# First products of a decoder step in another order, with their loads issued by two engines, and another order of the first head pair's units

## The chip, the cores and the metric

One core of one Trainium2 chip runs the whole program. The time is device microseconds of that core for one execution; less is better. The median of three runs of the kernel before is 1621.52 us.

## What is computed

One layer of a decoder step: 1,024 prompt tokens and 32 sample tokens (8 sequences of 4), model width 1,024. The reference, cut to what this case touches:

```python
d = x @ w_a_down                       # 1024 -> 384 (query) + 256 (latent) + 32 (rotary key)
c_q, c_kv, k_r = rms_norm(d[:384]), rms_norm(d[384:640]), rope(d[640:])
q = (c_q @ w_a_uq)                     # 16 heads of 64 + 32
k_nope = einsum('bsc,chd->bshd', c_kv, w_a_uk)
v      = einsum('bsc,chd->bshd', c_kv, w_a_uv)
p = softmax(mask((q_nope @ k_nope + q_rope @ k_r) * scale))
o = p @ v
```

The sample tokens attend to a paged cache in the latent space instead; then follow the output product, a layer norm, a gated ConvFFN and a second norm. Only the first 120 us of the program are touched here.

## The kernel before, in words

Products of prompt tokens are made of three matmuls each: both factors are split into a high part in a narrower format and the rest as a low part, and high x high, high x low and low x high are added in PSUM. ScalarE makes a high part (a copy) and VectorE the low part (a subtraction) out of it, so each operand goes through ScalarE, then VectorE. Weights, activations and intermediate results are all treated so. The eight PSUM banks are handed out by hand, and counters (semaphores) order the engines; each engine has its own list of instructions, in an order written out by hand, so a wait holds back all that stands behind it on that engine.

**project** (from L128). The 1,056 tokens are nine tiles (TILES): first the sample tile of 32 tokens, then eight of 128. For a tile, transpose_x turns x (eight transposes), ScalarE and VectorE split it, and `products` multiplies it with the down weight of 8 chunks k by 672 columns in two halves: six matmuls for a k. The sample tile is multiplied unsplit in down_samples: for each of the eight k, four matmuls side by side, each on a 32-column strip of the array, into bank 2. The first prompt tile (down_first) is multiplied while the weight's halves are made: its step k waits for chunk k to be split by ScalarE (L425) and VectorE (L513), and the next tile's transposes stand before step 6. SyncE issues the loads: the sample tile (128 KB), weight chunk 0 (336 KB), the first prompt tile (512 KB), chunks 1 to 7, and the next two x tiles. TensorE's list is: transposes of tiles 0 and 1, down_samples, down_first, transposes of tile 3, the next tile's products. At the end of the stage TensorE computes six units of the first head pair ahead ("early": v0, k0, q00, q10, q01, q11), each into its own bank.

**attend** (from L643). Eight head pairs, each with 16 score units; the projections of a pair are units too: v0, v1 (values transposed, 512 tokens each), k0, k1 (keys), q and two digits (head 0 or 1, third of the tokens 0, 1 or 2; one third is 352 columns, and third 2 has the sample tokens), wt (a transposed key weight), t0, t1 (values turned back), ql. A k unit is taken by ScalarE (k_hi, two copies) and VectorE (k_low, two subtractions); a q unit by VectorE (q_scale, out of the bank), ScalarE (q_high) and VectorE (q_low). q_high of third 2 has three small copies for the sample tokens before its own. The q units pass through two buffers, qf, in turn. For the first pair, FIRST is the order on TensorE, FIRST_TAKEN the order in which they are counted when taken, FIRST_BANK the bank and FIRST_AFTER the unit whose taking frees it. On entry TensorE computes wt, v1, k1, q02, q12, then scores(0, 0), which needs q02 split. The score unit n uses banks 0 and 1 for even n, 2 and 3 for odd n; scores of n = 2 need exp of n = 0. VectorE takes the row maximum, ScalarE the exponential.

```python
FIRST_BANK = {"v0": 0, "k0": 1, "q00": 4, "q10": 5, "q01": 2, "q11": 3, "wt": 6, "v1": 7, "k1": 1, "q02": 6, "q12": 0}
FIRST_AFTER = {"k1": "k0", "q02": "wt", "q12": "v0"}
```

## Time and profile before

| | |
|---|---|
| median of 3 runs | 1621.52 us (1621.4 to 1621.68) |
| profiled execution, its own time | 1620.46 us |
| its span in the trace | 1618.8 us |
| granted TensorE clock, mean | 0.998 |
| TensorE busy | 98% |
| VectorE, ScalarE, GpSimd busy | 58%, 36%, 12% |
| DMA, mean | 67 GB/s |

The span goes from the first to the last instruction. A busy share is an average; what a stretch is worth is read from the timeline of that stretch. In a timeline, "[1.62 <-DVE k_lo L1005]" behind an instruction says how long its engine was idle before it and which instruction's end released it. PE is TensorE's matmuls, PEld its weight loads, which overlap them; DVE is VectorE, ACT ScalarE, POOL GpSimd, SPq SyncE's queue.

### The profile page before, as it was taken

The numbers are of one execution on the slowest core, as the hardware profiler recorded it, in microseconds if no ns is written. First come the engines' busy times: TensorE is split into PE (matmuls) and PEld (weight loads), VectorE is DVE, ScalarE is ACT, GpSimd is POOL, SyncE is SP. The second block draws the span as 40 slices with busy tenths as digits, with TensorE's granted clock in tenths as the row PEclk, the third lists the DMA queues.
The fourth block names the chain that finished last, engine by engine and source line by source line (L and its number), as shares of the span: only waits on it lengthen the run. The fifth ranks groups of instructions, "written<-read, shape, count | busy, mean of one in ns | idle before, by whom it ended". The sixth has DMA issues, their size and how long they took to land. (4 is left out here: it accounts for less than half of the span.)

```text
span 1618.8 us, 29618 instructions
## 1 busy us (share of the span) xinstructions
PE 1584.5 (98%) x10341; PEld 1404.1 (87%) x10341; DVE 938.0 (58%) x1818; ACT 586.1 (36%) x1281; POOL 192.3 (12%) x297
## 2 busy tenths in 40 slices
PE   8989999999999999999999999999999999999998
PEld 7978888888886566657889999999999999999996
DVE  5665666656665655555766465545555554465547
ACT  5455655556554333332233131121302213131136
POOL 2000000000000430000003021120211202121000
PEclk9999999999999999999999999999999999999999
DMA  6111111011113765533113020220202112020103
GB/s 225 42 31 31 29 23 25 12 28 26 29 46 115 237 207 170 171 114 95 39 59 111 27 65 13 65 65 26 63 15 65 47 31 65 26 65 13 40 27 118
DMA packets 150583, 109.18 MB, mean 67 GB/s; under 512 B 54623, under 2 KB 139293, under 8 KB 150352
## 3 DMA queue, kind: packets, MB, share of 16 engines
q1 hardware_dynamic: 148704, 102.17, 21.4%
q0 software_dynamic: 1776, 5.71, 1.1%
q8 instruction: 56, 0.92, 0.2%
q14 instruction: 47, 0.39, 0.1%
HBM read 101.88 MB, written 10.14 MB: 69 GB/s over the span
## 5 line engine op out<-in xcount | busy, mean ns | idle before, releaser
L1950 PE MATMUL banks<-act_hi,up_hi 128*128 128x352 f32 (+2 forms) x1040 | 335.5, 323 | 0.7 <-PEq L1522 0.7
L1951 PE MATMUL banks<-act_lo,up_hi 128*128 128x352 f32 (+2 forms) x1040 | 335.1, 322 | 0.0
L1952 PE MATMUL banks<-act_hi,up_lo 128*128 128x352 f32 (+2 forms) x1040 | 334.9, 322 | 0.0
L1950 PEld LDWEIGHTS banks<-act_hi,up_hi 128*128 128x128 f32 x1040 | 195.5, 188 | 1.0 <-issue 0.9
L1951 PEld LDWEIGHTS banks<-act_lo,up_hi 128*128 128x128 f32 x1040 | 195.4, 188 | 0.0
L1952 PEld LDWEIGHTS banks<-act_hi,up_lo 128*128 128x128 f32 x1040 | 195.2, 188 | 0.0
L2253 DVE TENSOR_TENSOR o_t<-o_t,banks 128x352 f32<-128x352 f32 x240 | 121.0, 520 | 94.5 <-PE banks L1952 94.2
L2232 DVE SCALAR_TENSOR_TENSOR conv_out<-conv_in,conv_now,conv_out 128x1072 f32<-128x1072 f32 x42 | 63.7, 1517 | 185.7 <-ACT conv_out L2106 185.7
L1027 DVE TENSOR_REDUCE neg_max<-banks 128x1 f32<-128x896 f32 (+7 forms) x128 | 96.7, 756 | 115.6 <-PE banks L810 115.0
L2097 ACT ACTIVATE conv_in<-banks 128x352 f32<-128x352 f32 x84 | 36.2, 457 | 336.0 <-PE banks L1952 336.0
L1950 PE MATMUL banks<-gated_hi,down_hi 128*128 128x352 f32 x480 | 155.8, 325 | 0.0
L1951 PE MATMUL banks<-gated_lo,down_hi 128*128 128x352 f32 x480 | 154.3, 321 | 0.0
L1952 PE MATMUL banks<-gated_hi,down_lo 128*128 128x352 f32 x480 | 154.2, 321 | 0.0
L903 ACT ACTIVATE probs<-banks,neg_max 128x896 f32<-128x896 f32 (+7 forms) x128 | 94.5, 738 | 42.9 <-DVE inv_rows L1037 24.6
L1950 PEld LDWEIGHTS banks<-gated_hi,down_hi 128*128 128x128 f32 x480 | 90.1, 188 | 1.3
L1951 PEld LDWEIGHTS banks<-gated_lo,down_hi 128*128 128x128 f32 x480 | 90.2, 188 | 0.0
L1952 PEld LDWEIGHTS banks<-gated_hi,down_lo 128*128 128x128 f32 x480 | 90.1, 188 | 0.0
L821 PE MATMUL banks<-ident,probs 128*128 128x128 f32 x576 | 87.0, 276 | 2.6 <-DVE probs_t L1048 2.4
L732 PE MATMUL banks<-k_hi,q_hi 128*128 128x512 f32 (+2 forms) x192 | 71.9, 375 | 10.6 <-DVE q_scaled L1012 6.2
L839 PE MATMUL banks<-probs_t,v_rows 128*64 128x256 f32 (+1 forms) x640 | 72.8, 365 | 0.8 <-DVE probs_t L1048 0.8
L2235 DVE SCALAR_TENSOR_TENSOR conv_out<-conv_in,conv_now,conv_out 128x1072 f32<-128x1072 f32 x42 | 69.3, 1651 | 1.5
L821 PEld LDWEIGHTS banks<-ident,probs 128*128 128x128 f32 x576 | 62.0, 141 | 6.5 <-DVE probs_t L1048 4.4
(339 smaller groups left out, 3084.1 us busy)
## 6 DMA issues: line engine op xcount, KB each, us to landing
weight_stage<-in_w_f_up SPq DMA_DIRECT2D x44, 512.0 KB, 4.7
c_stage<-in_cache_kv_latent SPq DMA_DIRECT2D x140, 128.0 KB, 2.2
down_stage<-in_w_f_down SPq DMA_DIRECT2D x22, 512.0 KB, 4.3
head_weights_stage<-in_cache_kv_latent SPq DMA_DIRECT2D x56, 128.0 KB, 2.1
rope_query_tab<-in_cache_kv_latent SPq DMA_DIRECT2D x56, 128.0 KB, 2.2
o_t<-in_x_prompt SPq DMA_DIRECT2D x8, 512.0 KB, 4.2
rope_rows<-in_cache_k_rope SPq DMA_DIRECT2D x256, 16.0 KB, 1.9
wo_stage<-in_w_a_out POOLq DMA_DIRECT2D x8, 512.0 KB, 4.5
```

Source lines behind the costliest of these rows:

```text
L732: nc.tensor.matmul(o, ws[0], xs[0], start=first, stop=False)
L821: last = nc.tensor.transpose(ps[:, 4 + t % 2, k * P:(k + 1) * P], prob[:, n % 2, c + k * P:c + (k + 1) * P], m.ident[:, :])
L839: last = nc.tensor.matmul(ps[d, 6, q], v[:, j, d], pt[:, g % 2, hh, j, q], start=j == 0, stop=j == 2 * g + 1)
L903: nc.scalar.activation(prob[:, n % 2, 0:wd], src, ACT.Exp, bias=nmax[:, n % 2:n % 2 + 1], accum_out=sums[:, n % 2:n % 2 + 1]).then_inc(pr, 1)
L1027: nc.vector.tensor_reduce(nmax[:, n % 2:n % 2 + 1], src, axis=AXX, op=ALU.max, negate=True).then_inc(nm_ok, 1)
L1950: nc.tensor.matmul(o, ws[0], xs[0], start=first, stop=False)
L1951: nc.tensor.matmul(o, ws[0], xs[1], start=False, stop=False)
L1952: return nc.tensor.matmul(o, ws[1], xs[0], start=False, stop=last)
L2097: nc.scalar.activation(u[i][:, 2 + CH * c:2 + CH * c + CH], src, ACT.Copy).then_inc(ev, 1)
L2232: nc.vector.scalar_tensor_tensor(out=v[i][:, 0:CW], in0=u[i][:, 1:UW - 1], scalar=cwi[:, 1, i, j:j + 1], in1=v[i][:, 0:CW], op0=ALU.mult, ...
L2235: nc.vector.scalar_tensor_tensor(out=v[i][:, 0:CW], in0=u[i][:, 0:UW - 2], scalar=cwi[:, 0, i, j:j + 1], in1=v[i][:, 0:CW], op0=ALU.mult, ...
L2253: nc.vector.tensor_tensor(y, y, ps[:, 4 + unit % 4, 0:CH], ALU.add).then_inc(add, 1)
```

## The change

At the start, SyncE keeps the loads of the sample tile, of weight chunk 0 and of chunks 3 to 7; ScalarE issues those of the first prompt tile and of chunks 1 and 2, ahead of its first copy. On TensorE down_samples and down_first become steps of one k: after sample steps 0 to 4 prompt step 0 follows, then sample step 5, prompt step 1, and so on; prompt steps 4 to 7 come last.

At the entry of attention TensorE's order becomes wt, k1, q02, q12, v1, t0, scores(0, 0). k1 goes to v0's bank, q02 to bank 7, q12 to k0's bank, v1 to wt's bank. VectorE scales q01 and q11 first, before k0; it scales all q units before the first row maximum. ScalarE makes the high parts of q01 and q11 ahead of k1; the small copies for the samples move behind both high parts of third 2, and v1 is taken last. k_low's first half starts when the first half of k_hi is done. The scores wait for q02 alone (n = 0) and for q12 (n = 2).

```diff
--- before.py
+++ after.py
@@ -176,24 +176,25 @@
...
+        def load_x(eng, i):
+            t = TILES[i]
+            src = io["x_prompt"][0, t * P:(t + 1) * P, :] if t < TT - 1 else io["x_sample"].rearrange("b t d -> (b t) d")
+            eng.dma_start(x[0:rows(t), i % 2, :], src).then_inc(x_in[i % 2], 16)
+        def load_w(eng, k):
+            eng.dma_start(wst[k], io["w_a_down"][k * P:(k + 1) * P, :]).then_inc(w_in[k], 16)
...
-            def load_x(i):
-                t = TILES[i]
-                src = io["x_prompt"][0, t * P:(t + 1) * P, :] if t < TT - 1 else io["x_sample"].rearrange("b t d -> (b t) d")
-                sp.dma_start(x[0:rows(t), i % 2, :], src).then_inc(x_in[i % 2], 16)
-            def load_w(k):
-                sp.dma_start(wst[k], io["w_a_down"][k * P:(k + 1) * P, :]).then_inc(w_in[k], 16)
-            load_x(0)
-            load_w(0)
-            load_x(1)
-            for k in range(1, KD):
-                load_w(k)
+            load_x(sp, 0)
+            load_w(sp, 0)
+            for k in range(3, KD):
+                load_w(sp, k)
...
-                load_x(i)
+                load_x(sp, i)
...
@@ -206,7 +207,7 @@
...
-                    load_x(i + 3)
+                    load_x(sp, i + 3)
...
@@ -268,29 +269,29 @@
...
-            def down_samples():
-                pe.wait_ge(xt_hi, 2)
+            def down_samples(k):
+                pe.wait_ge(w_in[k], 16)
...
-                for k in range(KD):
-                    pe.wait_ge(w_in[k], 16)
-                    for g in range(4):
-                        last = nc.tensor.matmul(ps[32 * g:32 * g + 32, 2, 0:n], xs[:, k, :], wst[k][:, g * n:(g + 1) * n],
-                                                start=k == 0, stop=k == KD - 1)
-                last.then_inc(d_ps, 1)
-            def down_first():
-                pe.wait_ge(xt_hi, 4)
-                pe.wait_ge(xt_lo, 2)
-                for k in range(KD):
-                    if k == KD - 2:
-                        transpose_x(2)
-                    pe.wait_ge(w_hi, k + 1)
-                    pe.wait_ge(w_lo, k + 1)
-                    products(1, 0, k)
-                    last = products(1, 1, k)
-                last.then_inc(d_ps, 1)
+                for g in range(4):
+                    last = nc.tensor.matmul(ps[32 * g:32 * g + 32, 2, 0:n], xs[:, k, :], wst[k][:, g * n:(g + 1) * n],
+                                            start=k == 0, stop=k == KD - 1)
+                if k == KD - 1:
+                    last.then_inc(d_ps, 1)
+            def down_first(k):
+                if k == 0:
+                    pe.wait_ge(xt_hi, 4)
+                    pe.wait_ge(xt_lo, 2)
+                if k == KD - 2:
+                    transpose_x(2)
+                pe.wait_ge(w_hi, k + 1)
+                pe.wait_ge(w_lo, k + 1)
+                products(1, 0, k)
+                last = products(1, 1, k)
+                if k == KD - 1:
+                    last.then_inc(d_ps, 1)
...
@@ -341,8 +342,12 @@
...
-            down_samples()
-            down_first()
+            pe.wait_ge(xt_hi, 2)
+            for k in range(KD + 4):
+                if k < KD:
+                    down_samples(k)
+                if k >= 4:
+                    down_first(k - 4)
...
@@ -415,6 +420,9 @@
...
+            load_x(act, 1)
+            for k in (1, 2):
+                load_w(act, k)
...
@@ -538,8 +546,8 @@
...
-FIRST_BANK = {"v0": 0, "k0": 1, "q00": 4, "q10": 5, "q01": 2, "q11": 3, "wt": 6, "v1": 7, "k1": 1, "q02": 6, "q12": 0}
-FIRST_AFTER = {"k1": "k0", "q02": "wt", "q12": "v0"}
+FIRST_BANK = {"v0": 0, "k0": 1, "q00": 4, "q10": 5, "q01": 2, "q11": 3, "wt": 6, "v1": 6, "k1": 0, "q02": 7, "q12": 1}
+FIRST_AFTER = {"k1": "v0", "v1": "wt", "q12": "k0"}
...
@@ -590,8 +598,8 @@
...
-FIRST = ["v0", "k0", "q00", "q10", "q01", "q11", "wt", "v1", "k1", "q02", "q12", "t0", "t1", "ql"]
-FIRST_TAKEN = ["v0", "k0", "wt", "v1", "k1", "q02", "q12", "q01", "q11", "q00", "q10", "t0", "t1", "ql"]
+FIRST = ["v0", "k0", "q00", "q10", "q01", "q11", "wt", "k1", "q02", "q12", "v1", "t0", "t1", "ql"]
+FIRST_TAKEN = ["v0", "q01", "q11", "k0", "k1", "wt", "q02", "q12", "v1", "q00", "q10", "t0", "t1", "ql"]
...
@@ -658,6 +666,7 @@
...
+        qs_ok = s("q_samples_ok")
...
@@ -747,7 +756,7 @@
...
-                    bank_free(p, "q10" if p else "v1")
+                    bank_free(p, "q10" if p else "q02")
...
@@ -778,7 +787,7 @@
...
-                    pe.wait_ge(qn_ok, p + 1)
+                    pe.wait_ge(qn_ok, 2 * p + 2)
...
@@ -796,9 +805,9 @@
...
-                if n == 1 and p == 0:
-                    pe.wait_ge(pj_dve, dve_count(0, "q11"))
-                if n % 4 == 0 and g >= 1:
+                if n in (0, 2) and p == 0:
+                    pe.wait_ge(ql_ok, 3 + n // 2)
+                elif n % 4 == 0 and g >= 1:
...
@@ -858,6 +867,7 @@
...
+            project_unit(0, OWN_AT[0])
...
@@ -874,7 +884,7 @@
...
-                    if n in OWN_AT:
+                    if n in OWN_AT and p + n:
...
@@ -935,22 +945,24 @@
...
-                copy(m.khi[0:NOPE, 0, c], src[0:NOPE, :])
+                copy(m.khi[0:NOPE, 0, c], src[0:NOPE, :]).then_inc(kh_ok, 1)
...
+            def q_samples(p, name):
+                hh, i, at = int(name[1]), place_in(p, name, Q_UNITS) % 2, SEQ - 2 * CH
+                for part in range(2):
+                    r0 = (NOPE, 0)[hh] + part * ROPE
+                    copy(m.qr[0:ROPE, part, :, (2 * p + hh) * DEC_SEQ:(2 * p + hh + 1) * DEC_SEQ],
+                         qf[r0:r0 + ROPE, i, at:CH].rearrange("p (b t) -> p b t", t=DEC_SEQ)).then_inc(qs_ok, 1)
+                rows_ = slice(hh * NOPE, (hh + 1) * NOPE)
+                copy(qn[rows_, hh * N_SAMPLE:(hh + 1) * N_SAMPLE], qf[rows_, i, at:CH]).then_inc(qn_ok, 1)
...
-                if name[2] == "2":
-                    at = SEQ - 2 * CH
-                    for part in range(2):
-                        r0 = (NOPE, 0)[hh] + part * ROPE
-                        copy(m.qr[0:ROPE, part, :, (2 * p + hh) * DEC_SEQ:(2 * p + hh + 1) * DEC_SEQ],
-                             qf[r0:r0 + ROPE, i, at:CH].rearrange("p (b t) -> p b t", t=DEC_SEQ))
-                    rows_ = slice(hh * NOPE, (hh + 1) * NOPE)
-                    last = copy(qn[rows_, hh * N_SAMPLE:(hh + 1) * N_SAMPLE], qf[rows_, i, at:CH])
-                    if hh:
-                        last.then_inc(qn_ok, 1)
+                if name[2] == "2" and p:
+                    q_samples(p, name)
...
@@ -960,13 +972,17 @@
...
-            for name in FIRST_TAKEN[:len(EARLY) - 2]:
-                if name in BY_ACT:
-                    take(0, name)
-                elif name[0] == "k":
-                    k_hi(0, name)
-                else:
-                    q_high(0, name)
+            take(0, "v0")
+            k_hi(0, "k0")
+            q_high(0, "q01")
+            q_high(0, "q11")
+            k_hi(0, "k1")
+            take(0, "wt")
+            q_high(0, "q02")
+            q_high(0, "q12")
+            q_samples(0, "q02")
+            q_samples(0, "q12")
+            take(0, "v1")
...
@@ -998,10 +1014,12 @@
...
-                dve.wait_ge(kh_ok, 2 * p + place_in(p, name, ("k0", "k1")) + 1)
+                halves = 4 * p + 2 * place_in(p, name, ("k0", "k1"))
+                dve.wait_ge(kh_ok, halves + 1)
...
+                dve.wait_ge(kh_ok, halves + 2)
...
@@ -1009,6 +1027,9 @@
...
+                if p == 0 and name in ("q00", "q10"):
+                    dve.wait_ge(qn_ok, int(name[1]) + 1)
+                    dve.wait_ge(qs_ok, 2 * int(name[1]) + 2)
...
@@ -1059,19 +1080,19 @@
...
+            q_scale(0, "q01")
+            q_scale(0, "q11")
...
+            q_low(0, "q01")
+            q_low(0, "q11")
...
-            q_scale(0, "q01")
-            q_scale(0, "q11")
-            row_max(0, 0)
-            q_low(0, "q01")
-            q_low(0, "q11")
...
+            row_max(0, 0)
...

```

## Rows read from the trace of the kernel before

**Rows 1.** The page's busy part: share of the span that TensorE is busy.
```profile
PE 1584.5 (98%) x10341; PEld 1404.1 (87%) x10341; DVE 938.0 (58%) x1818; ACT 586.1 (36%) x1281; POOL 192.3 (12%) x297
```

**Rows 2.** TensorE's waits, whole span: us in total, times, longest us.
```profile
...
PE banks L732 <- DVE q_scaled L1012: 6.2, 7, 0.9
...
PE banks L732 <- DVE q_lo L1018: 3.3, 1, 3.3
...
PE banks L732 <- DVE k_lo L1005: 1.6, 1, 1.6
```

**Rows 3.** Busy time of PE, PEld, DVE, ACT, POOL; PEclk, DMA share, GB/s.
```profile
...
40.00:60.00 20.00, 20.00 (x145) 19.97 (x143) 12.81 (x57) 9.83 (x30) 0.00 (x0) 1.00 0.22 68
```

**Rows 4.** Timeline of the start, TensorE: start us, us, what, xcount.
```profile
6.37 1.97 PE L256 MATMUL banks<-ident,o_t 128*128 128x128 f32 x8 [1.72 <-DMA o_t<-in_x_prompt]
...
8.27 1.48 PEld L278 LDWEIGHTS banks<-o_t,x_samples_t 128*32 128x32 f32 x32 [0.33 <-ACT xt_hi_tile L380]
...
10.09 0.16 PEld L278 LDWEIGHTS banks<-o_t,x_samples_t 128*32 128x32 f32 x8 [0.34 <-DMA o_t<-in_w_a_down]
...
12.67 0.16 PEld L278 LDWEIGHTS banks<-rope_query_tab,x_samples_t 128*32 128x32 f32 x8 [0.68 <-DMA rope_query_tab<-in_w_a_down]
...
13.10 0.42 PE L267 MATMUL banks<-wdown_hi,xt_hi_tile 128*128 128x336 f32 x1
...
22.29 0.40 PE L267 MATMUL banks<-wdown_hi,xt_hi_tile 128*128 128x336 f32 x1
```

**Rows 5.** The same timeline, ScalarE and VectorE: the weight's halves.
```profile
8.87 3.37 ACT L425 ACTIVATE wdown_hi<-o_t 128x672 fp32r<-128x672 f32 x5
...
9.66 3.93 DVE L513 TENSOR_TENSOR wdown_lo<-o_t,wdown_hi 128x672 fp32r<-128x672 f32 x5
```

**Rows 6.** GB/s moved in 40 slices of 0.35 us, 0 to 14 us.
```profile
GB/s 0 0 0 0 0 187 125 232 123 300 320 388 327 363 413 386 346 307 269 307 399 376 407 384 346 384 438 384 415 438 384 430 412 422 394 433 410 421 421 375
```

**Rows 7.** The same timeline, SyncE's issue of the first prompt tile.
```profile
1.80 0.43 SPq L184 DMA_DIRECT2D o_t<-in_x_prompt  x1
```

**Rows 8.** Timeline of attention's entry, TensorE.
```profile
95.27 0.42 PE L767 MATMUL banks<-ident,head_weights_stage 128*128 128x128 f32 x2 [0.33 <-PEq L126]
...
98.71 0.50 PE L732 MATMUL banks<-ck_hi,wk_hi 128*128 128x512 f32 x1 [1.62 <-DVE k_lo L1005]
...
100.19 0.32 PE L732 MATMUL banks<-cq_hi,wq_hi 128*128 128x352 f32 x1
...
106.52 0.47 PE L732 MATMUL banks<-k_hi,q_hi 128*128 128x512 f32 x1 [3.26 <-DVE q_lo L1018]
...
107.88 0.45 PE L732 MATMUL banks<-k_hi,q_hi 128*128 128x512 f32 x1
...
109.38 0.61 PE L779 MATMUL banks<-ident,v_t 128*128 128x128 f32 x4
110.36 0.50 PE L732 MATMUL banks<-k_hi,q_hi 128*128 128x512 f32 x1 [0.37 <-ACT probs L903]
...
113.33 0.50 PE L732 MATMUL banks<-k_hi,q_hi 128*128 128x512 f32 x1 [0.65 <-ACT probs L903]
```

**Rows 9.** The same stretch, ScalarE.
```profile
95.95 1.18 ACT L893 ACTIVATE k_hi<-banks 64x512 fp32r<-64x512 f32 x2
...
103.60 0.47 ACT L893 ACTIVATE q_rope<-q_scaled 32x32 f32<-32x32 f32 x2 [2.01 <-DVE q_scaled L1012]
...
104.22 0.48 ACT L893 ACTIVATE q_hi<-q_scaled 128x352 fp32r<-128x352 f32 x1
...
109.21 1.01 ACT L903 ACTIVATE probs<-banks,neg_max 128x896 f32<-128x896 f32 x1
```

**Rows 10.** The same stretch, VectorE.
```profile
97.96 0.69 DVE L1005 TENSOR_TENSOR k_lo<-banks,k_hi 64x512 fp32r<-64x512 f32 x1
...
103.05 0.96 DVE L1012 TENSOR_TENSOR q_scaled<-banks,rope_query_tab 128x352 f32<-128x352 f32 x2
...
108.08 1.09 DVE L1027 TENSOR_REDUCE neg_max<-banks 128x1 f32<-128x896 f32 x1 [0.84 <-PE banks L810]
```

## Prediction

> **What bounds the kernel now.** I read the page first: TensorE is busy 98% of the span [rows 1], so time can only be won where it stands still. Its waits say where [rows 2]: 3.3 and 1.6 us once each, at one place, and 6.2 us in seven waits that come back in each later head pair, which the change leaves alone. The windows by stage show TensorE full from 40 to 60 us, 20.00 of 20.00 [rows 3]; the projection after the first prompt tile is TensorE's own work, so what is won ahead of it arrives at attention, and what is won at attention's entry arrives at the end, provided no other engine becomes late.
>
> The timeline of the start [rows 4] shows the first stretch. The prompt tile's transposes begin at 6.37, released by its load. The weight loads of the sample products begin at 8.27, and those of chunks 0 to 3 (32 loads) are through in 1.48 us; chunk 4's wait until 10.09 for its load, the last chunk's until 12.67, so the sample products follow the DMA. Only at 13.10 do the prompt tile's products begin. Yet their operands are there earlier [rows 5]: ScalarE splits chunk 0 from 8.87, VectorE from 9.66, five low halves in 3.93, so 0.79 each, and the first is ready at about 10.5.
>
> The second stretch is attention's entry [rows 8]: k1 waits 1.62 us for its bank, which VectorE frees by taking k0 until about 98.65 [rows 10]; the first scores wait 3.26 us for q02's low half; then 0.37 and 0.65 us for the first two exponentials. From 113.33 TensorE goes on with no wait of that size.
>
> **The start, step by step.** The number of instructions on TensorE stays. What changes is which of them fill the wait: prompt step 0 begins at a time F in place of 13.10. From 13.10 the eight prompt steps and two groups of transposes last until 22.29, 9.19 us [rows 4]. After the change three sample steps (5, 6, 7) lie in between. What one costs there is not in the trace; the bounds are 0.37 (1.48 / 4, steps back to back) and 0.85 (0.43, the isolated last step from 12.67 to 13.10, plus 0.42, one product that nothing overlaps, for emptying the array both ways). I take 0.53: the isolated step, plus the 0.10 by which the first product after it (0.42) is longer than a similar one in a stream (0.32, [rows 8]). That row is nearest, because it is the same change of shape. Sum: start gain = 13.10 - F - 3 x 0.53 = 11.5 - F.
>
> F is the later of two: the low half of chunk 0, and the end of sample step 4. Today they would be 10.5 and 10.09 + 0.43 = 10.5. Now the loads. ScalarE has nothing to do at the start and issues the prompt tile beside SyncE's first load, which is two issues (0.43 each, with a little between) ahead of 1.80 [rows 7]: 0.9 earlier. If transfer followed issue, everything behind it would be 0.9 earlier: F = 9.6. The DMA row speaks against it [rows 6]: from the slice at 3.15 us on it moves 300 to 430 GB/s without a hole, so the loads are limited by bytes there, not by issue. Up to 3.15 us it moved 0.35 x (187 + 125 + 232 + 123) = 233 KB, where the later rate would give about twice that; a second queue can fill half of that hole, about 0.4 us. So I put the prompt tile at 0.4 us earlier, and the halves of chunk 0 at 10.1.
>
> Chunks 1 and 2 stand behind the prompt tile on ScalarE's queue, while SyncE's goes on with 3, 4 and so on. With chunks 0 to 4, the sample tile and the prompt tile 2.3 MB are to be moved either way; chunk 2 was ready after 1.65 MB (128 + 512 + 3 x 336 KB), and if the two queues share evenly it is ready only after about 2.3 MB. At 400 GB/s that is 1.6 us later, less the 0.4. As chunk 4 (the 2.3 MB today) came at 10.09, chunk 2 comes at about 9.6, and sample steps 2, 3 and 4 follow it in 3 x 0.37: F = 10.6. ScalarE reaches chunk 2 at 8.87 - 0.4 + 2 x 0.67 = 9.8 and is not held back, nor is VectorE, whose low halves (0.79 each) run ahead of TensorE's prompt steps. **Start gain 0.9 us**; bounds 13.10 - 9.6 - 3 x 0.37 = 2.4 and, with chunk 2 at 10.1 and steps of 0.85, 13.10 - 11.2 - 2.55 = -0.7.
>
> By the Trainium skill (DMA: Bandwidth & Descriptors, "Queues, rings and completion order" and "Issuing engines are not separate DMA queues") SP's and ACT's loads share the same 16 engines, which take turns between the queues packet by packet, so a second issuer saves issue time only. By it chunk 2 comes late as above and the start gives about 0.9 us; by issue times alone it would give 13.10 - 9.6 - 1.6 = 1.9 us. Rows 6 side with the rule on the bytes; no row shows two such queues at once.
>
> The three DMA issues cost ScalarE 3 x 0.43 = 1.3 us in a stretch in which it waits for the first transposes anyway; only if its table load no longer fitted there would that cost something. SyncE is free earlier and issues the tile after next earlier; its bytes stand behind chunk 7 and are wanted only near 17 us. Edits at no cost: the second semaphore on k_hi, separate counts for the sample copies and the load helpers add no instruction that works, and in later pairs the order is the old one.
>
> **The entry of attention.** Times here are on the old scale. TensorE: wt at 95.27; k1 needs v0's bank, which ScalarE leaves when it turns to k0 at 95.95 [rows 9], so k1 at about 96.05 and 1.48 long [rows 8]; q02 and q12 1.46 each (100.19 to the end of both at about 103.1), v1 1.48 like k1, t0 0.5: scores(0, 0) can begin at 96.05 + 1.48 + 2.92 + 1.48 + 0.5 = 102.45. Nobody holds that up by more: VectorE scales q01 and q11 until 96.5 (0.96 a pair, [rows 10]), takes k0 behind ScalarE's halves (0.59 each) until 98.0, so q12's bank is free 1 us before TensorE wants it at 99.0; low halves of q01 and q11 until 98.95, k1 until 100.35 (1.39 for both halves), scales q02 and q12 until 101.3. ScalarE makes k1's high halves until 99.3 and takes wt at 99.65, so v1's bank is free 0.8 us early; then q02 high until 101.4 (0.48, without the 0.62 of sample copies that stood ahead of it, [rows 9]), and VectorE's q02 low half is done at about 102.0, 0.45 us ahead of TensorE. So v1 and t0, 1.98 us of work that was elsewhere, now cover this wait. Scores begin at 102.45 in place of 106.52: 4.07 us earlier.
>
> Then the maximum (108.08 today, 1.56 after the scores' start) at 104.0; VectorE's scales of q00 and q10 wait for the sample copies (two times 0.62 from 101.9) and end at 103.7, in time. The exponential (109.21) starts at 105.2, the third scores (110.36) at 106.3, and the fourth (113.33) at about 108.95, because the second maximum no longer stands behind two scale steps: **entry gain 4.2 us**, 4.07 to 4.4. As a check, the removed waits add to 1.62 + 3.26 + 0.37 + 0.65 = 5.9, and new ones of 0.5 (v0's bank), 0.9 and 0.4 (the exponentials) remain: 4.1. What is late next is the exponential, whose table load and row maximum end together. Bounds: 4.9 if one of the new waits goes too, 3.0 if TensorE stands 1.2 us at q02's low half, twice the handoff margin that I find.
>
> **Sum.** 0.9 + 4.2 = 5.1 us. The profiled execution took 1620.46, span 1618.8; it becomes 1615.4. The median of the runs stands 1.1 above it, 1621.52, so I say 1616.4. About 0.2%, 3.2 us, is what a measurement of this kernel can tell from no change.
>
> **Rivals.** (a) The start gives nothing, the entry all: chunk 2 late by the full 1.6 us and sample steps at 0.8; start between -0.7 and 0.4. For it: no row shows a mixed order of steps. Against it: prompt step 0 starts at least 1.9 us earlier in every bound. Time 1621.5 - 4.2 + 0.2 = 1617.5; 20%. The Trainium skill (TensorEngine Tiling (Array Packing), "Key Properties") says that a change of tiling mode drains TensorE, which is this rival's mechanism. (b) A handoff between ScalarE and VectorE stays at the entry, since seven follow one another there with margins under 1 us: entry 2.3, start 0.9, 1618.3; 11%. (c) Loads follow issue, and the sample steps are cheap: start 2, entry 4.3, 1615.2; 10%. (d) Slower than before: the DMA engines serve ScalarE's queue last. The prompt tile then lands behind 2.8 MB of SyncE's loads, at about 14 us instead of 6.37; prompt step 0 follows 4.1 us later at 18, with all chunks there: start 11.5 - 18 = -6.5, entry 4.2, time 1623.8. It decides against the change once the tile lands after 11.6 us. Against it: nothing in the rows, only that both queues are filled by the same kind of issue; 3%. (e) The gain doesn't reach the end, because a later stage hangs on loads or on GpSimd that start at fixed times: 1621; 3%. Against it, all loads there wait for TensorE's or VectorE's counts. The forecast itself has 53%.
>
> **How the numbers follow.** Cases (c), forecast, (a) and (b) span 1615.2 to 1618.3; with the bounds of the forecast (start 0.3 to 1.7, entry 3.7 to 4.6) 1615.2 to 1617.5. I give 1614.7 to 1618.6, leaving out (d), (e) and the tails of (a) and (b). Faster by over 0.2% means under 1618.3: the forecast, (c), most of (a) and about half of (b), 0.85; same 0.12; slower 0.03, half of (d) and what I don't see.
>
> **What would show it.** At the start: the prompt tile's transposes near 6.0; prompt step 0 between 10 and 11; three sample steps between prompt steps, 0.5 each; tile 2's products 0.9 earlier than 22.29. At the entry, against its own first instruction: k1 after 0.8 us, no idle time until the first scores 7.2 us after it, k1's bank wait and q02's low half gone from the list of waits, two exponentials still in it. If the first scores wait for q_lo, (b) holds; if prompt step 0 starts before 10, loads follow issue; if the transposes begin after 12, (d). I am wrong in the main if the entry gives under 3 us, or if the gain seen at 115 us is not there at the end.

## The result: 8.6 us less, where 5.1 were forecast

| | before | after |
|---|---|---|
| median of 4 runs each, one chip | 1621.58 us | 1612.98 us (1610.44 to 1613.67) |
| profiled execution, its span | 1620.46, 1618.8 us | 1613.67, 1612.0 us |
| granted TensorE clock, mean | 0.998 | 0.997 |

The ratio is 0.9947 (0.9934 to 0.9959). The change is faster, as forecast, but by more than the range of 1614.7 to 1618.6 us held.

The page's busy part of the kernel after has the instruction counts of [rows 1], nothing added or taken away, and TensorE at 98% as before:

```profile
PE 1586.9 (98%) x10341; PEld 1406.4 (87%) x10341; DVE 939.3 (58%) x1818; ACT 585.6 (36%) x1281; POOL 191.0 (12%) x297
```

TensorE's waits over the whole span of the kernel after (what was waited for: us in total, times, longest us):

```profile
PE banks L257 <- DMA o_t<-in_x_sample: 4.5, 1, 4.5
PE banks L830 <- DVE probs_t L1069: 2.3, 6, 0.4
PE banks L741 <- DVE q_scaled L1033: 1.9, 7, 0.3
...
PE banks L741 <- ACT probs L913: 1.3, 2, 1.1
PE banks L848 <- DVE probs_t L1069: 1.2, 1, 1.2
...
PE banks L741 <- ACT v_t L903: 0.4, 1, 0.4
PE banks L277 <- DMA o_t<-in_w_a_down: 0.4, 1, 0.4
```

Beside [rows 2]: the waits of 3.3 and 1.6 us are gone, as they should be. But the seven waits for q_scaled went from 6.2 to 1.9 us, and the forecast had them untouched.

**Where the time went.** I take four marks in the two traces and subtract. TensorE's first product of the third tile, 22.29 before and 21.65 after: 0.65 us won at the start. Attention from its first instruction on TensorE to decoding's first product (500.12 before, 491.99 after): 404.85 and 397.37, so 7.48 us won. From there to the first product of the next stage (742.48 and 735.66): 242.36 and 243.67, 1.31 lost. The rest is the same within 0.1 us, and TensorE is full from 40 to 60 us as in [rows 3]. 0.65 + 7.48 - 1.31 = 6.8, the difference of the spans. The medians differ by 8.6; a stretch at half clock that the profiled execution of the kernel before happens to lack may account for about one of the 1.8 us between them (part 2 of the experiments).

**The start**, TensorE's timeline of the kernel after (start us, us, what, xcount, idle time before and what released it):

```profile
9.17 1.49 PE L277 MATMUL banks<-o_t,x_samples_t 128*32 128x168 f32 x24 [0.37 <-DMA o_t<-in_w_a_down]
10.59 0.42 PE L268 MATMUL banks<-wdown_hi,xt_hi_tile 128*128 128x336 f32 x1
...
11.71 0.49 PE L277 MATMUL banks<-rope_query_tab,x_samples_t 128*32 128x168 f32 x8
12.13 0.42 PE L268 MATMUL banks<-wdown_hi,xt_hi_tile 128*128 128x336 f32 x1
...
21.65 0.40 PE L268 MATMUL banks<-wdown_hi,xt_hi_tile 128*128 128x336 f32 x1
```

Against [rows 4]: chunk 2 is late, its sample step waits until 9.17, and prompt step 0 begins at 10.59 instead of 13.10 (10.6 was forecast). Then each pair of a sample step and a prompt step takes 12.13 - 10.59 = 1.54 us, of which six products are 0.93 in a stream (11.16 - 10.85 is 0.31 for two of them), so a sample step in between costs 0.61 and not the 0.53 that I took. That prompt step 0 begins on time is in part luck: chunk 2 came 0.4 earlier than forecast, and the three sample steps behind it took 1.42 for 1.1. The queue of ScalarE issues the prompt tile at 0.87, for 1.80 in [rows 7]:

```profile
0.87 0.42 ACTq L183 DMA_DIRECT2D o_t<-in_x_prompt  x1
```

**Attention's entry**, the same view:

```profile
94.62 0.41 PE L776 MATMUL banks<-ident,head_weights_stage 128*128 128x128 f32 x2 [0.33 <-PEq L126]
95.45 0.50 PE L741 MATMUL banks<-ck_hi,wk_hi 128*128 128x512 f32 x1 [0.42 <-ACT v_t L903]
...
101.60 0.47 PE L741 MATMUL banks<-k_hi,q_hi 128*128 128x512 f32 x1
...
105.72 0.50 PE L741 MATMUL banks<-k_hi,q_hi 128*128 128x512 f32 x1 [1.09 <-ACT probs L913]
...
108.07 0.50 PE L741 MATMUL banks<-k_hi,q_hi 128*128 128x512 f32 x1
```

From its first instruction, k1 comes after 0.83 us, the first scores after 6.98 without a wait (11.25 before, [rows 8]), the fourth after 13.45 (18.06 before). ScalarE and VectorE show what is late next:

```profile
103.27 1.28 ACT L913 ACT_TABLE_LOAD   x1
104.56 1.01 ACT L913 ACTIVATE probs<-banks,neg_max 128x896 f32<-128x896 f32 x1
```
```profile
103.27 1.08 DVE L1048 TENSOR_REDUCE neg_max<-banks 128x1 f32<-128x896 f32 x1
```

The exponential starts when its table is loaded, 0.21 us after the row maximum is done; v1 was taken just ahead of the load. This is the 1.09 us of TensorE's wait.

**The boundary between two pairs**, which recurs seven times. VectorE and TensorE before:

```profile
154.28 0.68 DVE L1004 TENSOR_TENSOR k_lo<-banks,k_hi 64x512 fp32r<-64x512 f32 x1 [2.54 <-ACT k_hi L893]
154.97 0.69 DVE L1005 TENSOR_TENSOR k_lo<-banks,k_hi 64x512 fp32r<-64x512 f32 x1
...
156.47 0.95 DVE L1012 TENSOR_TENSOR q_scaled<-banks,rope_query_tab 128x352 f32<-128x352 f32 x2
```
```profile
157.03 0.50 PE L732 MATMUL banks<-k_hi,q_hi 128*128 128x512 f32 x1 [0.88 <-DVE q_scaled L1012]
```

ScalarE's two copies to k_hi there run from 153.05 for 1.20 us, and VectorE idles 2.54 us until both are done, although its first subtraction needs the first alone. Behind them stand an inverse, its copy and a step of o_t, and only then the scaling of q00, for which TensorE's next scores wait. After the change (the next boundary, VectorE, GpSimd and TensorE):

```profile
198.54 0.68 DVE L1021 TENSOR_TENSOR k_lo<-banks,k_hi 64x512 fp32r<-64x512 f32 x1 [1.94 <-ACT k_hi L903]
199.24 0.69 DVE L1023 TENSOR_TENSOR k_lo<-banks,k_hi 64x512 fp32r<-64x512 f32 x1
...
200.16 0.19 DVE L1058 COPY inv_rows<-inv_sums 128x64 f32<-128x64 f32 x1
...
200.72 0.94 DVE L1033 TENSOR_TENSOR q_scaled<-banks,rope_query_tab 128x352 f32<-128x352 f32 x2
...
201.77 0.75 DVE L1058 COPY inv_rows<-inv_sums 128x64 f32<-128x64 f32 x1
```
```profile
201.65 0.83 POOL L587 CAST wq_hi<-head_weights_stage 128x768 fp32r<-128x768 f32 x1
```
```profile
201.29 0.50 PE L741 MATMUL banks<-k_hi,q_hi 128*128 128x512 f32 x1 [0.27 <-DVE q_scaled L1033]
```

VectorE starts one copy, 0.60 us, earlier, and TensorE's wait falls from 0.88 to 0.27. The pair period (the distance from one pair's transposes of the key weight to the next pair's) is 50.59 before and 50.15 after.

**Behind attention** the windows (us; busy time of PE, PEld, DVE, ACT, POOL with counts; granted clock, DMA share, GB/s) show the loss, before and after:

```profile
500.00:501.00 1.00, 0.88 (x6) 0.87 (x6) 0.00 (x0) 0.00 (x0) 0.00 (x0) 0.90 0.00 0
501.00:504.00 3.00, 3.00 (x15) 2.94 (x16) 1.22 (x4) 1.04 (x4) 1.68 (x4) 0.50 0.78 243
504.00:505.00 1.00, 1.00 (x10) 1.00 (x9) 0.39 (x1) 0.57 (x1) 0.53 (x1) 0.89 0.91 293
```
```profile
491.00:492.00 1.00, 0.01 (x1) 0.04 (x1) 0.42 (x1) 0.14 (x1) 0.00 (x0) 0.69 0.00 0
492.00:498.00 6.00, 6.00 (x27) 5.87 (x28) 1.91 (x5) 1.61 (x4) 2.21 (x4) 0.50 0.72 216
498.00:499.00 1.00, 1.00 (x10) 1.00 (x9) 0.00 (x0) 0.92 (x2) 0.00 (x0) 0.90 0.84 252
```

TensorE waits for probs_t near the end of attention (0.78 us before, 1.15 after), then stands idle for 1.3 us at the change of stage, and works at half the clock (granted 0.50, 1.2 GHz) for about 3.4 us before and 6.8 us after: 1.7 and 3.4 us of work not done. The changed kernel's second trace (part 7) has 3.4. Of the 14 traces three show 6.8 us; all three have the new start, the new entry and the finer handoff, but four more of such kernels show 3.4. The stage then takes 243.2 to 243.7 us with the long stretch and 240.8 to 243.9 (mean 241.8) with the short one.

### The profile page after: what moved, and what is told of

It reads as the page before. It is cut to its first block and busy times, and to the rows that moved or that the text cites. A ratio compares the mean times of both kernels' runs of the same rounds, so it can differ in the third digit from the quotient of the medians.

```text
span 1612.0 us, 29621 instructions
## 1 busy us (share of the span) xinstructions
PE 1586.9 (98%) x10341; PEld 1406.4 (87%) x10341; DVE 939.3 (58%) x1818; ACT 585.6 (36%) x1281; POOL 191.0 (12%) x297
## 3 DMA queue, kind: packets, MB, share of 16 engines
q10 hardware_dynamic: 432, 1.21, 0.2%
```

## Experiments

The theory after the result: the unforecast part is the finer handoff in k_low, which is in the change for the entry but acts at every boundary. The first rival: the new entry order moves something in the later pairs. For the start: the order brings the gain, and the loads alone bring nothing; the rival is the reverse.

**1. The two parts of the start, alone.** The order without the loads:

```diff
             transpose_x(1)
-            down_samples()
-            down_first()
+            pe.wait_ge(xt_hi, 2)
+            for k in range(KD + 4):
+                if k < KD:
+                    down_samples(k)
+                if k >= 4:
+                    down_first(k - 4)
```

> The kernel before with the interleaved order of sample and prompt products alone; all first loads still from SyncE. Read at the first product of the third tile: 22.29 us in before, 21.65 with the whole change. Theory (the order brings the gain, its limit is the later of chunk 0's low half and sample step 4, the price is the mixed steps of 0.61 us each): prompt step 0 starts at 10.5, three mixed steps cost 1.8, so the third tile starts at 13.10 - 10.5 - 1.8 = 0.8 us earlier, at 21.5. Rival (the earlier prompt tile from the second queue brings it): no gain or a loss, 22.3 or later. The end of the program moves by the same amount, apart from the stage after attention.

Measured once: 1621.16 us (the kernel before beside it: median 1621.35 of 15 runs). Prompt step 0 at 11.35, the third tile at 22.41 (21.5 was expected): nothing won against 22.29. The same kernel again, later on:

> The interleaved order with all loads from SyncE, a second look. It gave 22.41 for the third tile, no gain, with prompt step 0 at 11.35. Theory now (third tile = prompt step 0 + 11.06, and prompt step 0 waits for chunk 4, which SyncE's loads alone bring at 10.0 to 10.7): between 21.5 and 22.5 again, where two issuers gave 20.8 to 22.1. Rival (the first look was an outlier and the order brings over 1 us): 21.3 or less.

1622.55 us; prompt step 0 at 10.79, the third tile at 21.92. The loads without the order:

```diff
-            load_x(0)
-            load_w(0)
-            load_x(1)
-            for k in range(1, KD):
-                load_w(k)
+            load_x(sp, 0)
+            load_w(sp, 0)
+            for k in range(3, KD):
+                load_w(sp, k)
...
+            load_x(act, 1)
+            for k in (1, 2):
+                load_w(act, k)
```

> The kernel before with the loads of the prompt tile and of chunks 1 and 2 issued by ScalarE, and the old order (all sample steps, then all prompt steps). Theory: the last chunk still comes when 3.3 MB have been moved, at 12.3 to 12.6 us, and the prompt steps start behind it, so the third tile starts within 0.3 us of 22.29; the first chunk's halves are ready 0.8 us earlier and wait. Rival (loads follow their issue): the last chunk 0.9 us earlier, third tile at 21.4.

1619.93 us; the last sample step begins at 11.67 (weights at 12.67 before, [rows 4]), prompt step 0 at 12.09, the third tile at 21.29, 1.0 earlier. The theory had it within 0.3 us of 22.29; the rival, 21.4, is what came. DMA's GB/s from 0 to 14 us in 40 slices of 0.35 us, with the loads from two queues, and then from one (the second run of the order alone):

```profile
GB/s 1 0 0 0 0 164 164 281 351 386 386 386 407 346 384 376 415 399 392 438 407 399 423 415 407 415 399 415 407 384 451 420 398 421 421 410 421 360 304 278
```
```profile
GB/s 0 0 0 0 0 176 187 189 108 361 401 417 410 433 314 361 315 223 215 323 384 346 361 415 369 384 422 399 399 438 384 407 446 407 436 445 398 398 445 434
```

With one queue the rate falls to 223 and 215 GB/s at 6 us (269 in [rows 6], at the same place); with two it stays between 346 and 438 from 2.8 to 10.5 us. This trace is among the best of its kind. Summed over the slices from 3.5 to 7 us, the traces of all runs give 1.16, 1.16, 1.19, 1.20 and 1.33 MB with one queue, and with two 1.28 (the changed kernel's own profile, with a dip of its own at 3.5 us) to 1.44, the mean of nine being 1.38. Up to 3.5 us two queues move no more (0.32 MB for 0.36, means), so by 7 us some 0.14 MB are won, a third of a microsecond's worth at 400 GB/s. What makes the single queue dip stays open.

How much of the start's gain is the order's and how much the loads' these runs don't settle, for TensorE's pace differs among them. In [rows 4] the eight transposes at 6.37 take 1.97 us; the eight of the same shape at 18.77 in the same trace take 1.04. The traces of the clock begin with its first record, and the views show 1.00 ahead of it for want of one; from the record on the products stand 0.16 us apart, and ahead of it 0.28 (rows of the changed kernel's second trace, in part 7). That record stands at 9.3 us in the kernel before, at 11.3 and 11.0 in the two runs of the order alone. There the first five sample steps run without a wait at the slow pace, the second time as

```profile
7.67 3.19 PE L278 MATMUL banks<-o_t,x_samples_t 128*32 128x168 f32 x40
```

and prompt step 0 follows them: TensorE itself was late, not chunk 4, for which [rows 4] has a wait. In the five traces of the changed start the record stands at 8.05, 8.33, 10.10, 11.42 and 12.84, and the third tile begins at 20.81, 21.11, 21.65, 22.12 and 22.86, in the same sequence. The two runs of the order alone (22.41 and 21.92) lie beside the one at 11.42. The old order waits for the last chunk with either pace. With two queues its sample step begins at 11.67, with one at 12.19, 12.67 and 13.02, 0.5 to 1.4 us later. The means, unchanged start 22.24, order alone 22.17, loads alone 21.29, are therefore not shares of one gain. With the old order the loads win in the one trace there is, and three sample steps at 0.61 (1.8 us) eat most of what an earlier prompt step 0 gives. What sets the time at which the clock rises stays open.

**2. The finer handoff, alone and left out.** Alone, on the kernel before:

```diff
-                copy(m.khi[0:NOPE, 0, c], src[0:NOPE, :])
+                copy(m.khi[0:NOPE, 0, c], src[0:NOPE, :]).then_inc(kh_ok, 1)
...
-                dve.wait_ge(kh_ok, 2 * p + place_in(p, name, ("k0", "k1")) + 1)
+                halves = 4 * p + 2 * place_in(p, name, ("k0", "k1"))
+                dve.wait_ge(kh_ok, halves + 1)
...
+                dve.wait_ge(kh_ok, halves + 2)
```

> The kernel before with one edit: k_low's first half starts when the first half of k_hi is done, in all eight pairs. Theory (this edit, which I costed at nothing, is the gain that I missed: VectorE takes k0 one ScalarE copy, 0.6 us, earlier, and TensorE's wait for q00's scale at the pair boundary is 0.88 us each time): the wait falls to 0.27 at seven boundaries, a pair lasts 50.15 in place of 50.59 us, and decoding starts 3 to 4 us earlier; time 1618 to 1619. In the first pair k1's wait for k0's bank falls by 0.6 too. Rival (it is worth nothing; the later gain comes from the different phase in which the first pair enters): 1621.5, waits of 0.88 as before.

1617.19 us (median of 9 runs; 1621.35 before; ratio 0.9968, 0.9958 to 0.9979): 4.2 us by an edit of four lines. The seven waits are 1.9 us in sum, the pair period is 50.16, attention is 3.10 us shorter than in the profile of the kernel before. At the first pair the scores come 1.05 us sooner, but the fourth stand at 18.10 us after attention's first instruction, for 18.06. What holds them up is the clock:

```profile
105.82 0.69 PE L732 MATMUL banks<-k_hi,q_hi 128*128 128x512 f32 x1 [2.82 <-DVE q_lo L1020]
106.31 0.63 PE L733 MATMUL banks<-k_lo,q_hi 128*128 128x512 f32 x1
106.74 0.63 PE L734 MATMUL banks<-k_hi,q_lo 128*128 128x512 f32 x1
```

These products stand 0.43 us apart, with a granted clock of 0.50 for 3.4 us from 105.9 on; in the profile before they stand 0.23 apart, at 1.00. The wait of about 3 us for q_lo lies just ahead of it. Of the five traces with the old entry four have such a stretch here (3.4 us in three, 6.8 in one), only the profile of the kernel before has none; of the nine with the new entry none has one. The two runs of the order alone have the old handoff and a stretch of 3.4 us: their fourth scores stand at 19.02 and 18.86 and their attention takes 405.77 and 405.68. Against them the handoff alone wins 4.0 us, in line with the 4.2 of the medians. By the same comparison the new entry wins 0.8 to 0.9 us more than the profile of the kernel before shows. How many of the executions without a profile have the stretch isn't known.

Left out, on the kernel after:

```diff
-                dve.wait_ge(kh_ok, halves + 1)
+                dve.wait_ge(kh_ok, halves + 2)
...
-                dve.wait_ge(kh_ok, halves + 2)
```

> The whole change, except that k_low waits for both halves of k_hi again, in all pairs. Theory: the boundaries wait 0.88 us seven times again and a pair lasts 50.59 us; the start and the entry keep their 0.65 and about 4.6 us, so decoding starts about 5 us earlier than in before and the time is 1616 to 1617, what I predicted for the whole. Rival: 1613, as the whole change.

1616.28 us (median of 7; ratio 0.9969, 0.9957 to 0.998). TensorE's waits:

```profile
PE banks L741 <- DVE q_scaled L1032: 6.2, 7, 0.9
```

The 6.2 us of [rows 2] are back, the pair period is 50.59, and attention is 3.58 us shorter than before. 3.58 + 3.90 for the handoff = 7.48. The rival falls: with the new entry and the old handoff the later pairs are as they were. And this kernel, the change without the term I missed, stands at the 1616.4 us that I forecast; partly by luck, as its own parts below are smaller in the traces (the start 0.5 us in the mean, the entry 3.6), and the clock at the entry can make up for it.

**3. The entry without the start.** The old project, the new entry of attention, k_low as in the last diff:

> The kernel before with the new order and banks of the first pair's units alone; the old start, and k_low waits for both halves. Theory (parts add up): from the first instruction of attention to the first scores 7.5 us as in the run without halves (11.25 in before), attention 3.6 us shorter in all, boundaries still 0.88, time 1621.4 - 3.6 = 1617.8. Rival (the entry's gain needs the half-wise taking of k0, for q12's bank): first scores 9 us or more after the first instruction.

1616.73 us (median of 10; 1621.24 before; ratio 0.9973, 0.9964 to 0.9983), attention again 3.58 us shorter (4.4 against the traces with the stretch at half clock; 1617.8 was expected for the time): first scores after 7.51 us (now with 0.29 of waiting for q_lo), the fourth after 14.06, so 4.0 us are won there. 0.37 of them are lost at attention's end: TensorE's last wait for probs_t is 0.78 us before and 1.15 in the kernels with the new entry. Why stays open. Beside the kernel of part 2 the whole new start changes the median by 0.5 us, less than these runs tell apart; their traces say 21.80 and 20.81 for the third tile.

**4. Why the pair is 0.44 shorter and not 0.61.** In the rows above VectorE's second copy to inv_rows takes 0.75 us; the first of the same shape takes 0.19, and before the change the longest is 0.20. It begins 0.12 us after GpSimd's large copy and ends 0.04 after it. The theory: the copy stands still for GpSimd's. Edit on the kernel after, GpSimd's copies of the next weights begin once the last inverse of the pair before is laid out, which is the copy in question:

```diff
                 pool.wait_ge(w.lo_ok, p + 1)
+                if p:
+                    pool.wait_ge(rb_ok, p * NU)
                 w.split_hi(nc, pool, p + 1)
```

> The whole change, with GpSimd's copies for the next pair held back until VectorE has made its last inverse copy of the pair before. In the changed kernel that copy takes 0.75 us once a pair, at the boundary, where GpSimd's first large copy runs; everywhere else 0.20. Theory (the copy waits for GpSimd's running copy, and that is why a pair is shorter by 0.44 us only, where TensorE's wait fell by 0.61): the copy takes 0.20 always, a pair lasts 49.98 to 50.02 in place of 50.15. Rival (the pair is held by something else): 50.15.

1611.04 us in one run; GpSimd's large copy now begins at 203.30, and VectorE's timeline has

```profile
202.10 0.20 DVE L1060 COPY inv_rows<-inv_sums 128x64 f32<-128x64 f32 x1
```

The pair period is 49.98, 0.17 less, attention 1.08 us shorter. Shown: the copy is long only where it runs beside GpSimd's, and the handoff moved VectorE's chain 0.6 us forward into GpSimd's copy, past whose last tenth of a microsecond it had slipped before. The Trainium skill (SBUF — State Buffer, "SBUF: two separate sides") says that an operation of VectorE that takes both port pairs, such as an fp32 copy from SBUF to SBUF, and one of GpSimd exclude each other for the whole instruction. The trace agrees: the 0.75 us end with GpSimd's 0.83.

**5. The 0.27 us that remain.** TensorE waits for q00's scaling before the next pair's first scores only since those of n = 1 need its bank. The wait moved there:

```diff
+                if n == 1 and p:
+                    pe.wait_ge(pj_dve, dve_count(p, "q00"))
...
-                    pe.wait_ge(pj_dve, dve_count(p + 1, "q00"))
                     scores(p + 1, 0)
```

> The whole change, with TensorE's wait for q00's scale moved from ahead of the first scores of a pair to ahead of the second ones, which are the first to write q00's bank. Theory (the remaining 0.27 us at each boundary is this wait): it disappears, k0's low half is there in time, a pair lasts 49.9 to 50.15 us, depending on how much of it VectorE's next row maximum gives back. Rival: the wait reappears as one of the same length for k0's low half or for the second scores, 50.15.

1610.28 us in one run. The period is 50.16 as before the edit; the wait has moved behind the scores:

```profile
202.41 0.87 PE L850 MATMUL banks<-probs_t,v_rows 128*64 128x256 f32 x8 [0.66 <-issue]
```

The product with the values now waits 0.66 us where the scores waited 0.27. The profile names no releaser, but in this run and in the changed kernel alike it starts 0.10 us behind the end of VectorE's copy to probs_t. So VectorE's chain behind q00 (inverse, the stalled copy, probs_t) is the limit, which part 7 bears out, and a wait taken away in front of it comes out behind it. Only the last periods and the way out of attention were 0.5 us shorter.

**6. The samples in two groups.** On the kernel after, one change of shape between products instead of three:

```diff
-            for k in range(KD + 4):
-                if k < KD:
-                    down_samples(k)
-                if k >= 4:
-                    down_first(k - 4)
+            for k in range(4):
+                down_samples(k)
+            for k in range(3):
+                down_first(k)
+            for k in range(4, KD):
+                down_samples(k)
+            for k in range(3, KD):
+                down_first(k)
```

> The whole change, with sample steps 0 to 3, prompt steps 0 to 2, sample steps 4 to 7, prompt steps 3 to 7. Theory (each switch between the two shapes costs about 0.25 us, 0.62 for a lone sample step against 0.37 in a row): prompt step 0 starts at 9.5 to 10.2, and the third tile starts 9.19 + 4 x 0.37 + 0.25 = 10.9 after it, 20.4 to 21.1, against 11.06 after it in the changed kernel, which started it at 10.6 and in another run at 9.75. Rival (loads decide): the third tile no earlier than 20.8 to 21.6 as with the change.

1612.88 us in one run. The third tile follows prompt step 0 by 10.66 us instead of 11.06, though four sample steps lie in between and not three. At full clock one takes 0.31 in a row (the second of the group starts 0.31 behind the first), so one group costs 1.47 = 4 x 0.31 + 0.23 on top of the 9.19 of the prompt steps, and three lone steps 1.87 = 3 x (0.31 + 0.31): a change of shape there and back costs 0.2 to 0.3 us. The third tile begins at 21.28, about 0.5 us earlier than the changed start's traces make likely at this one's clock (an estimate between 21.65 and 22.12); one run's time can't show it.

**7. Together.** The two groups, GpSimd later, and other banks at the entry (k1 in bank 7, which is free, q02 in v0's):

```diff
-FIRST_BANK = {"v0": 0, "k0": 1, "q00": 4, "q10": 5, "q01": 2, "q11": 3, "wt": 6, "v1": 6, "k1": 0, "q02": 7, "q12": 1}
-FIRST_AFTER = {"k1": "v0", "v1": "wt", "q12": "k0"}
+FIRST_BANK = {"v0": 0, "k0": 1, "q00": 4, "q10": 5, "q01": 2, "q11": 3, "wt": 6, "v1": 6, "k1": 7, "q02": 0, "q12": 1}
+FIRST_AFTER = {"q02": "v0", "v1": "wt", "q12": "k0"}
...
-                    bank_free(p, "q10" if p else "q02")
+                    bank_free(p, "q10" if p else "k1")
```

> The changed kernel with three edits: sample steps in two groups, GpSimd's copies held back as in the run with that edit alone, and k1 and q02 with their banks exchanged (k1 in bank 7, which is free, q02 in v0's bank), so that k1 need not wait for ScalarE's copy of v0. Theory (the parts add): k1 0.4 us earlier, pairs of 49.97 us, the start 0.4 us better at the same time of prompt step 0: attention 396.3 - 0.4 = 395.9 us, time 1.8 to 2 us under the changed kernel beside it. Rival: the 0.4 us at k1 is given back to the first exponential, whose table load ends the wait there: attention 396.3.

1610.36 us (median of 4; ratio 0.9932, 0.9916 to 0.9949). k1 no longer waits 0.42 us, but q_lo now makes the first scores wait 0.4: after 6.95 us instead of 6.98, nothing, as the rival had it (attention 396.27). The same with the moved wait of part 5:

> The same three edits and the late wait for q00's scale. That wait alone brought nothing, since the value products behind the first scores then waited 0.66 us for a copy of VectorE. Theory (that copy was late because VectorE stood behind GpSimd's copy, so both edits together bring what one alone can't): pairs of 49.7 us, attention 394 us, time 3 to 4 us under the changed kernel. Rival (that copy is late anyway, behind the two scale steps): pairs of 49.97 as without it.

1608.32 us (median of 4; 1607.55 to 1609.1; ratio 0.9918, 0.9902 to 0.9935). No wait for q_scaled is left, the period is 49.62, attention 393.62 us. What brought nothing to the period alone (50.16) brings 0.35 once GpSimd is out of VectorE's chain (49.97 to 49.62). The changed kernel beside these two:

> The changed kernel as it is, once more, as the measure for the two versions beside it and for how much its start and the stage after attention differ from run to run. Expected: prompt step 0 between 9.7 and 10.8, the third tile 11.06 us after it, attention 397.4 us from its first instruction to decoding's, as before; the median 1611.5 to 1613.5, lower where the stretch at half clock behind attention is 3.4 us long and not 6.8.

1613.55 us (median of 4; ratio 0.9952, 0.9935 to 0.9969; the first time 0.9947). The last kernel is 5.2 us faster still, and 13 us faster than the kernel before. Here prompt step 0 was at 10.95 and the third tile at 22.86, 0.8 later than the 11.06 behind it that was expected. The cause is TensorE's clock, of which this trace has the first record only at 12.84 us:

```profile
11.39 0.48 PE L269 MATMUL banks<-wdown_lo,xt_hi_tile 128*128 128x336 f32 x1
11.68 0.48 PE L270 MATMUL banks<-wdown_hi,xt_lo_tile 128*128 128x336 f32 x1
...
13.60 0.32 PE L269 MATMUL banks<-wdown_lo,xt_hi_tile 128*128 128x336 f32 x1
13.75 0.31 PE L270 MATMUL banks<-wdown_hi,xt_lo_tile 128*128 128x336 f32 x1
```

The products of prompt step 0 stand 0.28 us apart, those of step 1 0.16, as everywhere at full clock. In the first profile of the same kernel the clock was up at 10.10, ahead of prompt step 0.

## Why the prediction was right in sign and short in size

**The failed step** is the term costed at nothing: "Edits at no cost: the second semaphore on k_hi, separate counts for the sample copies and the load helpers add no instruction that works, and in later pairs the order is the old one." With it goes the reading of [rows 2]: "6.2 us in seven waits that come back in each later head pair, which the change leaves alone". The order is the old one, but k_low is called for every k unit of every pair. k0's halves are the first link of the chain that ends in those seven waits. The second half of that sentence was the argument for not following it. The term measures 4.0 us alone (3.1 against a trace without the stretch at half clock) and 3.9 on top of the new entry (7 x 0.44 in the later pairs, and in the first pair the fourth scores 0.61 earlier). It was to be had from the trace: VectorE 2.54 us idle at 154.28, released by the second k_hi, one copy 0.60 us long, times seven is 4.2 us; 3.1 arrive in the later pairs, for the 0.17 a pair of the copy that stands still.

**The entry** without that edit was 4.0 us to the fourth scores and 3.58 at attention's end; 4.2 was forecast, with the halves counted in. With them it is 4.6 to the fourth scores, above the term's 4.2 and inside its upper bound of 4.9. TensorE's own work ahead of the scores was 0.2 shorter than summed (v1 1.39 for 1.48, t0 0.36 for 0.5); the slack at q02's low half was smaller than forecast, some 0.25 and not 0.45. The two exponential waits stayed (1.3 us together), k1's bank wait was 0.42 for 0.5, the first scores came after 6.98 for 7.2. Rival (b) is out in the changed kernel; without the finer handoff it would have held at 0.3 us of its 1.9. A second term is missing from the sum: the old entry's wait for q_lo is followed by a stretch at half clock in four of five traces. The profile that I worked from is the fifth. "The median of the runs stands 1.1 above it" was carried over as if it were fixed, while the new entry has no such stretch in any trace; that is worth 0.8 to 0.9 us wherever it occurs.

**The start** came out at 0.65 us in the profiled pair for the 0.9 forecast; over the traces with each start the third tile's mean is 21.71 (5 traces, 20.81 to 22.86) against 22.24 (3 traces), 0.5 us. Prompt step 0's time was right in this trace (10.59; from 9.75 to 10.95 in the five); "I take 0.53" for a sample step should be 0.61, 0.25 us in sum. The 0.37 for a step "back to back" mixes two paces: some 0.6 at the slow one, 0.31 at the fast. The sum has no term for the clock, which in the old order cost nothing at the start and with which in the new one the third tile shifts by up to 2 us. The reasons for the loads' part did not hold. [rows 6] was read as moving "300 to 430 GB/s without a hole", but it falls to 269 at 6.3 us. That "a second queue can fill half of that hole" ahead of 3.15 us did not come true: up to 3.5 us two queues moved no more. "The loads are limited by bytes there, not by issue" did not hold either: with two queues more bytes move between 3.5 and 7 us, where [rows 6] seemed full. The rule of the Trainium skill cited with that term (DMA: Bandwidth & Descriptors, "Issuing engines are not separate DMA queues": a second issuer saves issue time only) is neither borne out nor refuted: the gain in bytes lies 2 us and more behind the first issues, but with two issuers SyncE's issue of the last chunks ends at 4.51 (loads alone) and not at 6.01, which is just ahead of the dip. Chunk 2 late: right (9.17 for 9.6). Rivals (c) and (d) are out; (a)'s start of -0.7 to 0.4 was not what came, but its mechanism, dear sample steps, took 1.8 of 2.5 us.

**The sum.** 0.65 + 7.48 - 1.31 in the profiles. By the marks the forecast's own parts gave 0.65 + 3.58 = 4.2 for 5.1, the missed one 3.9. The 1.31 behind attention is, as far as the traces tell, the longer stretch at half clock: 1.7 us more than before in this trace. For the medians, with the entry and the handoff taken against traces that have the stretch at the entry, the parts are 0.5 + 4.4 + 3.9 = 8.8 us (an estimate), for 8.6 and, the second time, 7.7 measured. No rival had the miss, since all of them varied terms in the sum, and this one was not in it. As the range was built from those terms alone, it could not hold the time.

## What to carry to other kernels

- An edit in a helper acts at every call. Before it is costed at nothing, count its callers and look whether one stands in a chain that ends in a recurring wait; a small wait times its repeats can outweigh the large one that the change is about.
- Where one engine's work is handed on in pieces, let the next start at the first piece; and when a chain is moved forward, look what else it now runs beside.
- A wait removed in front of the engine that sets the pace comes out behind it. Try such an edit again after that engine's chain is shortened.
- Take more than one trace before comparing stretches: one of the two may hold a stretch at half clock that the other lacks, and a gain then looks given back.

## What the runs showed of the hardware

- VectorE's 128x64 fp32 copy, 0.20 us, took 0.75 while GpSimd's 128x768 copy ran; with GpSimd's copy moved, 0.20 again.
- The same loads issued by two engines moved 1.38 MB (mean of nine traces) from 3.5 to 7 us, by one 1.21 (mean of five), which shows a dip near 6 us; up to 3.5 us they moved no more.
- At full clock a sample step (32-column strips) between full products costs 0.61 us, against 0.31 in a row of such steps; in the first 8 to 13 us, before the clock is up, some 0.6 in a row.
- At the start TensorE runs at half its pace (products of 336 columns 0.28 us apart, later 0.16) until 8.05 to 12.84 us, in different executions of nearly the same kernels. The changed start's third tile follows it, from 20.81 to 22.86.
- Behind a wait of 2.8 to 3.3 us at attention's entry the clock is halved for 3.4 or 6.8 us in four of five traces; that costs 0.8 to 1.2 us of attention.
- Behind attention the clock is halved for about 3.4 or 6.8 us; of the traces of one and the same kernel after, the first shows 6.8 (3.41 us lost) and the second 3.4 (1.71 lost). A single profile's time is not to be read closer than these 1.7 us.
